# Turning the last retention head's rows inside the first output unit of a retention and sparse attention step

## The reference, cut to what matters

```python
def retention_mixer(h, s0, w_in, gn_g, w_out):
    proj = h @ w_in
    q, k, v, g = jnp.split(proj, [RET_QK, 2 * RET_QK, 2 * RET_QK + RET_V], axis=-1)
    ...
    o, s_fin = retention(q, k, v, s0)      # S_t = gamma S_(t-1) + k_t^T v_t, o_t = q_t S_t
    o = head_layernorm(o.transpose(0, 2, 1, 3), gn_g).reshape(B, T, RET_V)
    return (o * jax.nn.silu(g)) @ w_out, s_fin
```

## Time and profile before

| what | value |
|---|---|
| median of 3 runs | 649.01 us (647.47 to 649.75) |
| the profiled execution's own time | 649.95 us |
| span of the profiled execution | 648.2 us, mean granted TensorE clock 0.981 |
| PE busy | 607.0 us, 94% |
| DVE busy | 363.7 us, 56% |
| ACT busy | 237.6 us, 37% |
| POOL busy | 214.7 us, 33% |
| moved by DMA | 190.30 MB, mean 294 GB/s |

### The profile page before, as it was taken

One profiled execution on the slowest core, in us unless ns is written; L12 is line 12 of the kernel. 1 busy time (PEld: TensorE's weight loads), 2 busy tenths in 40 slices (PEclk: granted clock), 3 DMA queues, 4 the chain that ended last, 5 costly groups with the idle time before them and its releaser, 6 DMA issues. The chain is left out here.

```text
span 648.2 us, 11421 instructions
## 1 busy us (share of the span) xinstructions
PE 607.0 (94%) x4335; PEld 379.8 (59%) x4335; DVE 363.7 (56%) x726; ACT 237.6 (37%) x488; POOL 214.7 (33%) x242
## 2 busy tenths in 40 slices
PE   6899999999999999979999999999989988759996
PEld 5566656775676567543567657777644555534441
DVE  2343747466745674455524814436797955874822
ACT  3355343624451454222334335454053245231010
POOL 1061128022603340312481369999711021110010
PEclk9999999999999999998999999999999998789998
DMA  8997384996789488984793745436999999999982
GB/s 300 380 383 269 132 274 157 328 383 220 244 311 374 159 300 314 387 329 163 265 382 132 268 150 191 176 133 207 358 403 407 408 407 408 408 399 410 400 344 82
DMA packets 82370, 190.30 MB, mean 294 GB/s; under 512 B 4167, under 2 KB 12631, under 8 KB 82316
## 3 DMA queue, kind: packets, MB, share of 16 engines
q1 hardware_dynamic: 80484, 183.71, 76.5%
q0 software_dynamic: 1296, 4.46, 2.2%
q10 hardware_dynamic: 536, 1.41, 0.6%
HBM read 167.14 MB, written 22.41 MB: 292 GB/s over the span
## 5 line engine op out<-in xcount | busy, mean ns | idle before, releaser
L553 POOL TENSOR_TENSOR weights_low<-ring,weights_high 128x512 fp32r<-128x512 f32 x96 | 123.8, 1324 | 74.5 <-PE bank L800 39.7
L1398 ACT ACTIVATE weights_high<-ring 128x1024 fp32r<-128x1024 f32 x84 | 86.2, 1054 | 85.9 <-PE bank L819 58.0
L811 PE MATMUL bank<-weights_high,h_high 128*128 128x512 f32 x272 | 109.6, 403 | 0.0
L811 PE MATMUL bank<-weights_high,h_low 128*128 128x512 f32 x272 | 107.2, 394 | 0.0
L819 PE MATMUL bank<-weights_low,h_high 128*128 128x512 f32 x272 | 82.9, 406 | 0.2 <-POOL weights_low L553 0.2
L811 PEld LDWEIGHTS bank<-weights_high,h_high 128*128 128x128 f32 x272 | 51.0, 188 | 25.9 <-issue 15.0
L553 DVE TENSOR_TENSOR weights_low<-ring,weights_high 128x512 fp32r<-128x512 f32 x72 | 45.5, 688 | 27.8 <-PE bank L800 16.4
L811 PEld LDWEIGHTS bank<-weights_high,h_low 128*128 128x128 f32 x272 | 51.2, 188 | 10.8
L819 PEld LDWEIGHTS bank<-weights_low,h_high 128*128 128x128 f32 x272 | 48.5, 189 | 11.9 <-issue 2.2
L1986 DVE SCALAR_TENSOR_TENSOR ring<-ring,bank 128x512 f32<-128x512 f32 x64 | 41.8, 685 | 15.3 <-PE bank L994 11.8
L2112 DVE STREAM_TRANSPOSE ring<-ring 128x1024 f32<-128x1024 f32 x40 | 46.2, 1213 | 5.4 <-DMA ring<-in_cache_k 5.3
(11 more groups left out here) (272 smaller groups left out, 1014.8 us busy)
## 6 DMA issues: line engine op xcount, KB each, us to landing
ring<-in_w_ada SPq DMA_DIRECT2D x12, 2048.0 KB, 13.6
ring<-in_cache_k SPq DMA_DIRECT2D x40, 512.0 KB, 8.7
ring<-in_cache_v SPq DMA_DIRECT2D x40, 512.0 KB, 10.1
ring<-in_w_ret_in SPq DMA_DIRECT2D x8, 2048.0 KB, 13.2
ring<-in_state_ret SPq DMA_DIRECT2D x32, 512.0 KB, 9.8
out_state_sample<-ring SPq DMA_DIRECT2D x32, 512.0 KB, 7.5
ring<-in_w_moba_in SPq DMA_DIRECT2D x8, 2048.0 KB, 8.6
arena<-in_cache_k SPq DMA_DIRECT2D x24, 512.0 KB, 10.9
```

The lines of the kernel that those rows point to most:

```text
L553: tensor_tensor(w_low[:, slot, k, :], ring[:, slot, k * CH:(k + 1) * CH], high[:, k, :].bitcast(F32), ALU.subtract).then_inc(low_ready[LOW ...
L811: pe.matmul(o[i][:, :], xs[p][i][:, k, :], high[:, k, :], start=k == 0 and p == 0, stop=False)
L1398: nc.scalar.activation(w_high[u[0] == "moba"][:, 2 * i:2 * i + 2, :].rearrange("p a b -> p (a b)"), w[:, 2 * i * CH:(2 * i + 2) * CH], ACT ...
```

## The change

In `bank_plan` the two modulation pieces of head 3 swap banks 4 and 5, and with them that head's part and its third row tile: the third row tile is now in bank 5 and the part in bank 4, as in the other heads. The three turns of head 3 stand ahead of the new-state products in the plan. On PE, the turns go one each behind the first, second and third plain product; the four groups of new-state products go behind products 4, 7, 10 and 13. The wait for ACT's copies stays in front of `out_samples(0, 1)`. On ACT, the copies of the turned rows and their rounding stand ahead of the rounding of unit (0, 1)'s weights.

```diff
--- before.py
+++ after.py
@@ -192,7 +192,7 @@
     def ada(layer, chunks):
 
         for i, c in enumerate(chunks):
-            use(("part", "ada", layer, c), 5 - i % 2)
+            use(("part", "ada", layer, c), 4 + i % 2)
             if i:
                 pair(("mod", layer, chunks[i - 1], 0), ("mod", layer, chunks[i - 1], 1))
         pair(("mod", layer, chunks[-1], 0), ("mod", layer, chunks[-1], 1))
@@ -232,14 +232,14 @@
         if h in ADA_AT:
             ada(0, ADA_GATE)
 
-        use(("part", "o", h), 5 if h in ADA_AT else 4)
+        use(("part", "o", h), 4)
         pair(("row", "o", h, 0), ("row", "o", h, 1))
-        use(("row", "o", h, 2), 4 if h in ADA_AT else 5)
+        use(("row", "o", h, 2), 5)
         misc(("S", h, 0))
         misc(("S", h, 1))
-    news(RH - 1)
     for n in range(3):
         misc(("yT", RH - 1, n))
+    news(RH - 1)
     project(("rout", 0))
     use(("part", "rout", 1), 4)
     k = 2 * (turn["pair"] % 2)
@@ -1076,16 +1076,21 @@
                     pe.wait_ge(kd_ready, 2 * h + 2)
                     js = slice(j * P, (j + 1) * P)
                     sealed(by_parts(o, [(kd_high[:, n, js], kd_low[:, n, js], n) for n in range(2)]), ("S", h, j))
-            def last_head_turned():
-                turn_y(RH - 1)
+            def of_last_head(i):
+                if i in (1, 2, 3):
+                    turn_y(RH - 1, (i - 1,))
+                if i in (4, 7, 10, 13):
+                    new_four(RH - 1, i // 3 - 1)
+
+            def last_head_there():
                 for n in range(3):
                     wait_read(pe, ("yT", RH - 1, n))
 
 
             assert (RH - 1) * DV >= D and 2 * NS == 2 * KT
             out_samples(0, 0)
-            out_plain(0, 0, lambda i: i % 4 == 0 and new_four(RH - 1, i // 4))
-            last_head_turned()
+            out_plain(0, 0, of_last_head)
+            last_head_there()
             out_samples(0, 1)
             out_split(0, 1)
             add_groups(("rout", 0))
@@ -1492,10 +1497,10 @@
 
             wait_full(act, ("S", RH - 1, 1))
             y_rounded(RH - 2)
-            high_weights(("rout", 0, 1), range(4))
             for n in range(3):
                 turned(L0["yT"][:, 4 * RH - 4:4 * RH, :], ("yT", RH - 1, n), n)
             y_rounded(RH - 1)
+            high_weights(("rout", 0, 1), range(4))
             copy_part(("rout", 0))
             act.wait_ge(half_used, 1)
             y_rounded(0)
```

## The result

| | before | changed |
|---|---|---|
| median of the runs beside each other, us | 648.62 (4: 647.47 to 649.75) | 644.19 (4: 643.10 to 646.13) |
| ratio, 95% interval | | 0.9933 [0.9908, 0.9957] |
| profiled execution, its span, us | 649.95, 648.2 | 646.13, 644.3 |
| the same change in a later set, us | 649.06 (20 runs) | 645.31 (11), ratio 0.9945 [0.9928, 0.9963] |

A forecast was written before the change was run, and what follows sets the result against it. PE was taken to bound layer 1's projections, transfers the attention behind. Terms -3.10 - 1.69 - 0.91 + 0.99 + 0.70 sum to -4.01; the walk's 4.05 was taken: 649.01 - 4.05 = 645.0 us, range 642.8 to 648.0.

The forecast's parts named there:

- The wait of 3.10 us for bank 4: PE before the first sample rows, waiting for DVE's third row tile: the bank swap removes it, 3.10 us less.
- The clock, 1.69 us: First sample rows on PE: without the gap the clock stays at 2.4 GHz, 1.92 us instead of 3.61.
- slower, by the clock: Rival: 1.2 GHz granted from the first turn's new wait to the tile's end, 8.8 us doubled, 653.8 us; chance 0.04.
- The two waits for ACT, 0.91 us: PE at the turns: ACT's copies are done long since, so waits of 0.34 and 0.57 us go.
- The new wait of the first turn: PE behind the first plain product, waiting for DVE's S copies to free bank 6: 0.99 us more, bounds 0 and 3.10.
- The new wait of the third group: PE at the third group of new-state products, waiting for DVE to free the fourth bank: 0.7 us more, bounds 0 and 3.2.
- The walk: Step along PE from 289.30 to the second sample rows: they start at 310.70 instead of 314.75, 4.05 us earlier.
- DVE and POOL: DVE's rest of head 3's rows and POOL's rests of weights miss each other by 0.24 us: cost 0, bounds 0 to 1.5.
- The loads: Loads of units (1, 0), (1, 1) and layer 1's first piece land in time: cost 0, bounds 0 and 1.0.
- What is late next: Layer 1's first piece, queued behind two modulation pieces, lands at 347.5 where 347.83 is needed: margin 0.3 us.
- Handed on: From second sample rows to program end: the 4.05 us carry through in full; rival, only in part, 646.2 to 647.2, chance 0.16.

The follow-up runs named there:

- one turn later: The changed kernel with each turn of head 3 one product later on PE and the new-state groups moved later too: 643.41 us, ratio 0.9922.
- the kernel with the wait filled: The kernel before, with 11 unused identity products on PE in an idle bank ahead of the first sample rows: 646.85 us, ratio 0.9970.

## Why the prediction was right

The forecast was 645.0 us, in 642.8 to 648.0; 644.19 was measured, and 645.31 in the later set. Point by point, in the order of its steps:

- **The wait of 3.10 us for bank 4** is gone with the swap and stays without it; the order has no part in it. The rows start 0.33 us after the start of the last S product, which is 0.40 long.
- **The clock, 1.69 us**, was right: 3.61 to 1.92, and 1.69 again when only the idle time was filled. The rival "slower, by the clock" did not come: the granted clock is 1.00 in every 5 us from 285 to 320.
- **The two waits for ACT, 0.91 us**, are gone. Undoing the swap leaves just this and the new wait of the third group; it gained 0.44.
- **The new wait of the first turn** was predicted as 0.99, counted from start to start. So counted it measured 1.08. The 0.81 in brackets is shorter, since it begins only with the end of the product's record (292.15, where the walk has 292.06). PE had the bank at 292.96 (293.05), DVE's copies having begun 0.11 earlier.
- **The new wait of the third group** measured 0.55, predicted 0.70. DVE was through with group 2 at 303.90 (300.71 and 3.19). With the 0.15 of handover that the prediction takes, the bank was there at 304.05, and PE went on to the next product 0.33 after that, where I had added the 0.43 of a whole group.
- **The walk** gave 310.70; it was 310.36. With the 0.14 from upstream taken off it is 4.25 us instead of 4.05. The 0.2 is in the three turns, which take 1.33 us by starts where the walk gives them 3 times 0.52. Two smaller misses cancel: the third group's wait is 0.16 shorter, and each of the four stretches of three products takes 2.77 us and not 2.73.
- **DVE and POOL** miss each other by 0.17 us (0.24 by my times), and POOL took 11.99, as forecast. The value I took, 0, was right by that margin alone: one turn later, the meeting cost 0.97 us of POOL's time, inside the 0 to 1.5 given for it. That it came out at 0 is in part luck. And one reading was wrong: the 10.50 us of the earlier trace rows that I took for POOL alone had one of DVE's additions beside it (L1950 at 332.74, 1.07 us instead of 0.69). Alone it is 10.06, so two subtractions cost 1.93 and not 1.5.
- **The loads.** Unit (1, 0) was issued at 308.45 (308.8), unit (1, 1) at 322.30 (322.17), layer 1's first piece at 338.92 (339.25), and ACT had it at 347.70 (347.5, in 347 to 348.5). "What is late next" was the right one: it costs nothing here, and was the bound when PE gained 1.6 to 2.4 us more before it, in kernels where the load was late by 0.6 to 1.2 us as well.
- **Handed on.** 4.25 us locally, 4.24 at layer 1, 4.19 at the first keys (4.33 less the 0.14 from upstream). At the very end it is 3.83 by the profiled executions, and 3.6 and 4.3 by the two ratios (0.9945 and 0.9933). The differences behind layer 1 are smaller than the scatter told of below.

What the prediction did not say is that the halves don't add. Of the two new waits the one for the S copies belongs to the swap (2.40 us with the swap alone, 1.08 with both), the one of the third group to the order (it stands there with the order alone: 1.07 us at 306.83). The order's larger part is that it shortens the first.

## What to carry to other kernels

When a wait for an engine is removed, look at what that engine releases next and put work between that doesn't need it; here that was worth 1.36 of 4.25 us, more than the waits that the reordering itself removes. A wait long enough to bring the clock down costs more than its length (here 3.10 and 1.69), and filling it wins back the second part even when the first can't be. And write down the margins of the covers, not only that they hold: 0.17 us of one and a load just in time decided what further edits were worth. Where one engine's work is held back, look at what of its later work now falls beside the other engine.

## What the runs showed of the hardware

**The end of the program has two lengths.** From the issue of the y stores of the prompt rows to that of the sample rows (L671) it is 24.0 us in five profiled executions and 25.6 to 25.7 in eight, with nothing between, whatever the change. The profiled executions of before and of the change are both of the longer kind. PE in order of time at the end of the change, and of the kernel with the wait filled:

```profile
632.77 2.68 PE L1219 MATMUL bank<-ring,h_turned 128*32 128x512 f32 x16 [0.75 <-DVE h_turned L2290]
635.21 2.90 PE L1219 MATMUL bank<-modulation,h_turned 128*32 128x512 f32 x16
```

```profile
635.08 1.92 PE L1216 MATMUL bank<-ring,h_turned 128*32 128x512 f32 x16 [0.75 <-DVE h_turned L2287]
636.82 1.90 PE L1216 MATMUL bank<-modulation,h_turned 128*32 128x512 f32 x16
```

Busy time from 635 to 640 us in the same two (the last three numbers are clock, DMA share, GB/s):

```profile
635.00:640.00 5.00, 5.00 (x24) 1.24 (x16) 0.76 (x2) 1.19 (x2) 0.00 (x0) 0.78 0.00 0
```

```profile
635.00:640.00 5.00, 4.92 (x35) 1.54 (x36) 0.21 (x2) 1.19 (x2) 0.00 (x0) 1.00 0.00 0
```

The same last products are done partly at 1.2 GHz in the one and wholly at 2.4 in the other, behind the same two waits for DVE (0.75 us in the row, and 1.06 and 1.07 just before) and the same busy time of PE in those 4 us, 2.19. These 1.7 us are two fifths of what this change brought. They are enough for single executions of one kernel to stand that far apart, and may be part of why the medians of the table follow layer 1 only to about 1 us; that link wasn't tried. What decides which of the two an execution gets was not tried.

**Idle time and the clock.** Around the change, the sample rows behind 3.10 us of idle time took 3.61 and 3.39 us instead of 1.92; after 0.64 and 1.11 us of it they and their like took 1.92, and after 0.81 us the products behind the first turn lost nothing. At the end of the program the level fell in the one execution of the two above and not in the other, behind the same waits, none of them as long as 3.10.

**What DVE and POOL take from each other.** POOL pays 0.97 us for each subtraction of DVE beside it, which alone takes 1.22; the steps are so even (10.06, 11.03, 11.99, 12.96) that they can be counted from POOL's total. For additions half as long (L1955, 0.69 us alone) it pays half as much: 10.49, 10.9 and 11.32 us beside one, two and three. DVE pays too: 0.81 us on one subtraction, 1.97 on two.
